# First normalisation of a hybrid encoder kernel: the inverse norms moved from a scaling pass into a diagonal matrix used in the turn

## The chip, the cores and the metric

One NeuronCore of one Trainium2 chip runs the whole program. The metric is the device time of one execution in microseconds (us), and the number that counts is the median over several runs. The engines are named PE (TensorE, matrix products; PEld is its weight load), DVE (VectorE), ACT (ScalarE), POOL (GpSimd) and SP (SyncE, which only issues transfers here).

## The reference, cut to what matters

```python
def rmsnorm(x, g):
    xf = x.astype(F32)
    y = xf * lax.rsqrt(jnp.mean(xf * xf, axis=-1, keepdims=True) + EPS)
    return (y * g.astype(F32)).astype(x.dtype)

def encoder_layer(x, mem, P, l):
    ...
    u = rmsnorm(x, P['norm_mix'][l])
    proj = u @ P['w_in'][l]
    ...
```

The model is one encoder layer on two groups of rows, 1024 prompt rows and 256 sample rows, each 1024 channels wide, in float32. What comes after the lines above (differential attention, a Hyena convolution, gates, cross-attention and a mixture of 16 experts) is not touched by the change. The first thing that the layer does is `u = rmsnorm(x, norm_mix)`: each row of `x` is divided by the root of its mean square and each channel is multiplied by a gain.

## The kernel before, in words

The rows of both groups form ten tiles of 128 rows (NT = 10). Most of the program is a long run of matrix products that want their inputs with channels on partitions. So the first stage must produce `UT`, the normalised and turned input: 8 blocks of 128 channels by 1280 rows. It starts from `XS`, in which the ten tiles lie as they come from memory, rows on partitions.

For each tile t the stage does five things, each on the engine that has it:

- SP loads the rows, two tiles to a transfer (`x_load`, line 429), ahead of the weights and tables that the next stages read. The transfers of the filter network's inputs and weights (`feat_in`, lines 452 to 455) and of the first projection weights (`hyena_load`, line 448) come behind them in the same queue.
- ACT squares the tile and sums it by row (line 1417), then takes the root of the mean (line 1419). This is `normed`; it counts in `norm_act`.
- DVE takes the reciprocal of the root (line 1739) and multiplies the tile's 1024 columns by it into one of two buffers `XN` (line 1745). This is `scaled`; it counts in `xn_ready`.
- PE turns the eight 128x128 blocks of `XN`, four into each of the banks 6 and 7 (`turn_rows`, line 763). The block is the stationary side and the identity matrix the moving one. It counts in `xn_tr`, one for each half.
- DVE multiplies each half (128x512) by the channels' gains on its way out of the bank into `UT` (`rows_in`, line 1752), which counts in `ut_ready`.

The order on DVE is written out in `norm_stage`: scaling of tile t+1 first, then the two halves of tile t. PE may turn half h of tile t+1 once DVE has emptied half h of tile t. DVE may write a buffer of `XN` once the turn of two tiles earlier is done with it.

```python
            wait("feat_in", 64)
            wait("ut_ready", 2 * NT)
            for n in range(3):
                filter_layer(0, n)
            for b in range(2 * HG):
                wait(f"hy_in_{b % 3}", 16 * (b // 3 + 1))
```

These lines (841 to 846) are what PE does next: it waits for the filter's inputs and for all twenty halves, does the first layer of the filter network (three products, line 747), and goes on to the projections of the Hyena branch (line 747 too, the line of the helper `product`). `norm_stage` is used for this first stage alone here; the later normalisations call `scaled`, `turn_rows` and `rows_in` themselves and are unchanged.

Of the kernel before, what the change touches and what calls it, by code (L numbers as in the profile page):

```python
# [11 lines left out]
ALU = mybir.AluOpType  # L12
# [3 lines left out]
P = 128  # L16
# [5 lines left out]
NT = NTP + NTS  # L22
# [22 lines left out]
V_MIX, V_X, V_MEM, V_FFN = 0, 8, 16, 24  # L45
# [62 lines left out]
class Count:  # L108
# [12 lines left out]
    def wait(self):  # L121
        self.eng.wait_ge(self.sem, self.base + self.n)
# [28 lines left out]
def encoder_kernel(nc, a, out_p, out_s):  # L151
# [9 lines left out]
    with ExitStack() as ctx:  # L161
        sem = {n: ctx.enter_context(nc.semaphore(n)) for n in SEMS}
        arena = ctx.enter_context(nc.sbuf_tensor("arena", [P, 204 * 256], F32))
        PS = ctx.enter_context(nc.psum_tensor("banks", [P, 8, 512], F32))

        def at(kb, *dims):

            n = int(np.prod(dims))
            v = arena[:, int(kb * 256):int(kb * 256) + n]
            if len(dims) == 2:  # L170
                v = v.rearrange("p (a b) -> p a b", a=dims[0])
            if len(dims) == 3:
                v = v.rearrange("p (a b c) -> p a b c", a=dims[0], b=dims[1])
            return v

        def small(name, shape, dt=F32):
            return ctx.enter_context(nc.sbuf_tensor(name, shape, dt))

        vec, ident, mirror = small("vec", [P, NV]), small("ident_sb", [P, P]), small("mirror_sb", [P, P])
        ones, eps = small("ones", [P, 2]), small("eps", [P, 1])  # L180
        stat = small("stat", [P, 3, 16])
# [13 lines left out]
        UT = at(0, KD, T)  # L195
        XS = at(80, NT, D)
        XN = [at(194 + 4 * i, D) for i in range(2)]
        SQJ = at(202, D // 2).bitcast(BF16)
        FEAT, H1, ARG, RND, H2 = at(60, T), at(65, T), at(70, T), at(75, T), at(140, T)
        W3F, W1F, W2F, VROW = at(145, 2 * HY), at(149, P), at(149.5, P), at(150, P)  # L200
# [75 lines left out]
        def bank4(b):  # L276
            return PS[:, b, :].rearrange("p (a c) -> p a c", a=4)

        def wide(v, n):

            return v.unsqueeze(2).to_broadcast([v.shape[0], v.shape[1], n])
# [44 lines left out]
        tiles = [slice(t * P, (t + 1) * P) for t in range(NT)]  # L326
# [96 lines left out]
        def _(sp):  # L423
# [146 lines left out]
            for t in range(NT):  # L570
# [3 lines left out]
                sp.wait_ge(sem["xn_ready"], N_FFN + t + 1)  # L574
                sp.dma_start(hn[tiles[t], :], XN[t % 2]).then_inc(sem[f"hn_out_{t % 2}"], 16)
                if t == NTP - 1:
# [166 lines left out]
        def _(pe):  # L743
            def product(out, pairs):

                for n, (l, r) in enumerate(pairs):
                    last = pe.matmul(out, l, r, start=(n == 0), stop=(n == len(pairs) - 1))  # L747
                return last

            def wait(name, v):  # L750
                pe.wait_ge(sem[name], v)
# [4 lines left out]
            def turn_rows(q):  # L756

                wait("xn_ready", q + 1)
                for half in range(2):
                    if q >= 1:  # L760
                        wait("ut_ready", 2 * (q - 1) + half + 1)
                    for k in range(4):
                        last = pe.transpose(PS[:, 6 + half, k * P:(k + 1) * P], XN[q % 2][:, tiles[4 * half + k]], ident[:, :])  # L763
                    last.then_inc(sem["xn_tr"], 1)

            for t in range(NT):
                turn_rows(t)

            def filter_layer(layer, n):

# [120 lines left out]
            for g in range(HG):  # L891
# [14 lines left out]
                for odd in range(2):  # L906
                    last = product(PS[:, 5, odd * P:(odd + 1) * P],
                                   [(KSS[:, 2 * odd + s, tiles[g]], INVS[:, 2 * odd + s, :]) for s in range(2)])
# [264 lines left out]
            for q in range(8):  # L1173
                m, n = q % 4, q // 4
# [134 lines left out]
            for m in range(NTP // 2):  # L1309
                last = pe.transpose(PS[0:2 * NE, 2, m * P:(m + 1) * P],  # L1310
                                    LG[:, 2 * m:2 * m + 2, :].rearrange("p h e -> p (h e)"), ident[:, :])
# [13 lines left out]
            for m in range(NTS):  # L1325
                last = pe.transpose(PS[0:NE, 5, m * P:(m + 1) * P], LG[:, NTP + m, :], ident[:, :])
# [82 lines left out]
        def _(act):  # L1409
            steps = Count(act, sem["norm_act"])  # L1410

            def normed(q, src):

                col = q % 16
                if q:
                    steps.wait()
                steps.inc(act.activation(SQJ, src, ACT.Square, accum_out=stat[:, 0, col:col + 1]))
                steps.wait()
# [268 lines left out]
            def fin_square(t):  # L1687
                act.wait_ge(sem[f"fin_in_{t // 2}"], 16)
                if t:
                    fin.wait()  # L1690
                fin.inc(act.activation(SQJ, FIN[t], ACT.Square, accum_out=stat[:, 0, t:t + 1]))

# [11 lines left out]
            act.wait_ge(sem["fin_rec"], 1)  # L1704
            fin.inc(act.activation(SQJ[:, 0:256], YS, ACT.Square, accum_out=LSUM[:, 0:1]))
            act.wait_ge(sem["fin_rec"], 2)
            fin.wait()
            fin.inc(act.activation(SQJ[:, 0:512], YP[:, 0:512], ACT.Square, accum_out=LSUM[:, 1:2]))
            act.wait_ge(sem["norm_mm"], 2)
            fin.inc(act.activation(LSUM[:, 3:4], PS[:, 0, 0:1], ACT.Sqrt, scale=1.0 / D, bias=eps[:, 0:1]))  # L1710
            act.wait_ge(sem["fin_rec"], 3)
            fin.wait()
            fin.inc(act.activation(SQJ[:, 512:1024], YP[:, 512:1024], ACT.Square, accum_out=LSUM[:, 2:3]))
            act.wait_ge(sem["fin_rec"], 4)
# [4 lines left out]
        def _(dve):  # L1719
# [11 lines left out]
            step = Count(dve, sem["dve_step"])  # L1731
# [3 lines left out]
            def scaled(q, src, stored):  # L1735

                dve.wait_ge(sem["norm_act"], 2 * q + 2)
                col = slice(q % 16, q % 16 + 1)
                step.inc(dve.reciprocal(stat[:, 2, col], stat[:, 1, col]))
                if q >= 2:  # L1740
                    dve.wait_ge(sem["xn_tr"], 2 * (q - 1))
                if stored and q >= N_FFN + 2:
                    dve.wait_ge(sem[f"hn_out_{q % 2}"], 16 * ((q - N_FFN) // 2))
                step.wait()
                dve.tensor_scalar(XN[q % 2], src, stat[:, 2, col], None, ALU.mult).then_inc(sem["xn_ready"], 1)

            def rows_in(q, dst, t, gain):

                for half in range(2):
                    dve.wait_ge(sem["xn_tr"], 2 * q + half + 1)  # L1750
                    g = vec[:, gain + 4 * half:gain + 4 * half + 4]
                    dve.tensor_tensor(dst[:, 4 * half:4 * half + 4, tiles[t]], bank4(6 + half), wide(g, P), ALU.mult).then_inc(sem["ut_ready"], 1)  # L1752

            def norm_stage(q0, n, src, dst, gain, stored=False):
                scaled(q0, src(0), stored)
                for t in range(n):
                    if t + 1 < n:
                        scaled(q0 + t + 1, src(t + 1), stored)
                    rows_in(q0 + t, dst, t, gain)

            norm_stage(0, NT, lambda t: XS[:, t, :], UT, V_MIX)

            def angles(layer):

# [118 lines left out]
            half = [HALF[:, m, :] for m in range(4)]  # L1883
# [41 lines left out]
            for g in range(HG):  # L1925
# [4 lines left out]
                for odd in range(2):  # L1930
                    for s, bank, c0, c1, o, n in ((0, 3 + odd, 0, 512, 0, LP), (1, 5, odd * P, (odd + 1) * P, LP, LS)):
                        dst, src = Z[:, g, o + odd:o + n:2], PS[:, bank, c0:c1]
                        if not odd and not s:
                            dst, src = dst.rearrange("p (i r) -> p r i", r=2), src.rearrange("p (r i) -> p r i", r=2)
# [248 lines left out]
            for q in range(8):  # L2183
                m, n = q % 4, q // 4
# [200 lines left out]
            for j in range(4):  # L2385
                if j:
                    step.wait()
                src = ident[:, CS * j:CS * (j + 1)]
# [13 lines left out]
            last = NE - 1  # L2402
# [40 lines left out]
def build(nc, arrays):  # L2443
    a = {n: nc.dram_tensor(f"in_{n}", v.shape, F32, kind="ExternalInput").ap() for n, v in arrays.items()}
    outs = [nc.dram_tensor(f"out_{i}", s, F32, kind="ExternalOutput").ap() for i, s in enumerate(_OUTS)]
    encoder_kernel(nc, a, *outs)
# [11 lines left out]
```

## Time and profile before

| | us |
|---|---|
| median of 3 runs | 2751.53 (2748.62 to 2759.06) |
| the profiled execution's own time | 2748.56 |
| its span, first to last instruction | 2746.8 |
| PE busy | 2641.3 (96%) |
| DVE busy | 878.5 (32%) |
| ACT busy | 418.1 (15%) |
| POOL busy | 251.4 (9%) |
| first product of the stage after the first normalisation | starts at 33.19 |

The profiled execution took 1.8 us more than its span, which is what lies before the first and behind the last instruction. It lies 3.0 us below the median of the three runs and beside the lowest of them. Times in the trace count from the span's start. A matrix product's duration covers its way through the array, so that successive ones overlap: the spacing of a group of n is (the group's time less one duration) / (n - 1).

### The profile page before, as it was taken

The numbers are of one execution on the slowest core, as the hardware profiler recorded it, in microseconds if no ns is written. First come the engines' busy times: TensorE is split into PE (matmuls) and PEld (weight loads), VectorE is DVE, ScalarE is ACT, GpSimd is POOL, SyncE is SP. The second block draws the span as 40 slices with busy tenths as digits, with TensorE's granted clock in tenths as the row PEclk, the third lists the DMA queues.
The fourth block names the chain that finished last, engine by engine and source line by source line (L and its number), as shares of the span: only waits on it lengthen the run. The fifth ranks groups of instructions, "written<-read, shape, count | busy, mean of one in ns | idle before, by whom it ended". The sixth has DMA issues, their size and how long they took to land.

```text
span 2746.8 us, 29882 instructions
## 1 busy us (share of the span) xinstructions
PE 2641.3 (96%) x12380; PEld 1780.4 (65%) x12380; DVE 878.5 (32%) x1512; ACT 418.1 (15%) x946; POOL 251.4 (9%) x270
## 2 busy tenths in 40 slices
PE   7999899999989999999999999978999999999997
PEld 4554454466657777765455486546888788788876
DVE  5566733166782111144200053271111111111112
ACT  3120000144451111102100032110000000000002
POOL 0120100000001010041000002000100110010001
PEclk9999999999999999999999999978999999999999
DMA  4110211000010010041111100137787787778776
GB/s 156 31 50 3 91 51 31 0 16 1 1 47 24 23 47 23 24 168 31 46 46 31 61 31 31 62 123 272 256 278 248 240 272 265 262 234 271 248 260 245
DMA packets 189938, 315.78 MB, mean 115 GB/s; under 512 B 6122, under 2 KB 69951, under 8 KB 189216
## 3 DMA queue, kind: packets, MB, share of 16 engines
q1 hardware_dynamic: 181952, 292.87, 31.1%
q0 software_dynamic: 7904, 21.76, 3.1%
q8 instruction: 58, 0.95, 0.1%
q14 instruction: 24, 0.20, 0.0%
HBM read 288.40 MB, written 26.21 MB: 115 GB/s over the span
## 4 chain that ended last, share of the span: by engine, by line
PE 90%; DVE 8%; ACT 1%; issue 1%; DMA 0%; POOL 0%; POOLq 0%; DVEq 0%; SPq 0%; ACTq 0%
PE banks L747 60%; PE banks L1029 9%; PE banks L928 5%; PE banks L1118 4%; PE banks L1243 3%; PE banks L948 2%; PE banks L1378 2%; DVE arena L1895 2%; PE banks L963 1%; PE banks L763 1%; PE banks L1348 1%; DVE arena L1752 0%; DVE arena L2279 0%; DVE arena L2282 0%; DVE att L1995 0%
## 5 line engine op out<-in xcount | busy, mean ns | idle before, releaser
L747 PE MATMUL banks<-arena 128*128 128x160 f32 (+3 forms) x8070 | 1754.2, 378 | 23.5 <-ACT arena L1449 8.1
L747 PEld LDWEIGHTS banks<-arena 128*128 128x128 f32 x8070 | 1245.9, 191 | 536.5 <-issue 479.4
L1029 PE MATMUL banks<-arena 128*128 128x320 f32 x896 | 243.5, 433 | 2.6 <-DVE arena L2031 2.1
L633 POOL TENSOR_TENSOR arena<-arena 128x512 f32<-128x512 f32 (+1 forms) x72 | 109.6, 1535 | 1294.8 <-DMA arena<-in_w_br_hyena 749.9
L1029 PEld LDWEIGHTS banks<-arena 128*128 128x128 f32 x896 | 169.7, 190 | 72.5 <-issue 2.3
L2362 DVE TENSOR_TENSOR arena<-arena,banks 128x160 f32<-128x160 f32 x128 | 41.1, 321 | 521.1 <-ACT arena L1679 488.7
L1679 ACT ACTIVATE arena<-banks 128x160 f32<-128x160 f32 x120 | 36.5, 304 | 773.2 <-PE banks L747 773.2
L928 PE MATMUL banks<-arena 128*128 128x512 f32 (+1 forms) x384 | 142.7, 521 | 2.5 <-DVE arena L1935 2.5
L1118 PE MATMUL banks<-arena 128*128 128x512 f32 x280 | 122.6, 593 | 0.7 <-ACT arena L1589 0.7
L1995 DVE TENSOR_REDUCE att<-banks 128x1 f32<-128x1024 f32 (+1 forms) x80 | 81.4, 1059 | 125.4 <-PE banks L948 125.3
L928 PEld LDWEIGHTS banks<-arena 128*128 128x128 f32 x384 | 70.5, 190 | 55.4 <-issue 52.4
L1243 PE MATMUL banks<-arena 128*128 128x512 f32 x224 | 100.8, 605 | 0.0
L1511 ACT ACTIVATE arena<-banks,att 128x1024 f32<-128x1024 f32 (+1 forms) x80 | 78.8, 986 | 116.6 <-DVE att L1995 116.6
L1118 PEld LDWEIGHTS banks<-arena 128*128 128x128 f32 x280 | 52.2, 190 | 61.8 <-issue 60.3
L948 PE MATMUL banks<-arena 64*128 64x512 f32 (+1 forms) x288 | 69.2, 594 | 13.1 <-ACT arena L1511 12.3
L2370 DVE TENSOR_SCALAR arena<-banks,gates 128x512 f32<-128x512 f32 x30 | 22.5, 751 | 173.4 <-PE banks L747 173.4
L1243 PEld LDWEIGHTS banks<-arena 128*128 128x128 f32 x224 | 43.0, 196 | 50.3 <-issue 50.3
L707 POOL TENSOR_TENSOR turn<-ones 128x1 f32<-128x1 f32 x15 | 2.9, 195 | 642.3 <-DVE arena L2373 642.3
L2176 DVE COPY arena<-banks 128x512 f32 (+1 forms) x8 | 5.5, 692 | 174.4 <-PE banks L747 174.4
L1378 PE MATMUL banks<-arena 128*32 128x256 f32 x1024 | 58.6, 380 | 0.8 <-DVE arena L2362 0.8
L948 PEld LDWEIGHTS banks<-arena 64*128 64x128 f32 x288 | 24.6, 186 | 51.6 <-issue 39.2
L2093 DVE TENSOR_TENSOR arena<-arena,banks 128x512 f32<-128x512 f32 x40 | 27.5, 687 | 88.9 <-PE banks L747 88.9
(241 smaller groups left out, 1596.7 us busy)
## 6 DMA issues: line engine op xcount, KB each, us to landing
arena<-in_w_exp_gate SPq DMA_DIRECT2D x32, 2048.0 KB, 8.0
arena<-in_w_exp_up SPq DMA_DIRECT2D x32, 2048.0 KB, 12.9
arena<-in_w_exp_down SPq DMA_DIRECT2D x32, 2048.0 KB, 18.1
arena<-in_w_in SPq DMA_DIRECT2D x36, 512.0 KB, 4.0
arena<-in_x_prompt SPq DMA_DIRECT2D x8, 1024.0 KB, 7.7
residual_rows<-arena SPq DMA_DIRECT2D x10, 512.0 KB, 2.6
normed_rows<-arena SPq DMA_DIRECT2D x10, 512.0 KB, 2.6
arena<-residual_rows SPq DMA_DIRECT2D x5, 1024.0 KB, 15.3
```

Source lines behind the costliest of these rows:

```text
L633: done.inc(pool.tensor_tensor(out, l, r, op))
L747: last = pe.matmul(out, l, r, start=(n == 0), stop=(n == len(pairs) - 1))
L928: last = pe.matmul(PS[:, job_bank(h, j), n * cn:(n + 1) * cn], WQK[h][part][:, k, :], UT[:, k, c0:c0 + cn], start=(k == 0), stop=(k == KD ...
L948: last = pe.matmul(PS[:, 2 * c + n // 512, 0:m], q[half, tiles[i]], k[half, k0 + n:k0 + n + m], start=True, stop=True, tile_position=(c * ...
L1029: last = pe.matmul(PS[:, 3 * (g % 2) + bank, 0:GN], l[:, k, :], r[:, k, :], start=(k == 0 and which in (G1, G2, G5)), stop=(k == 3), skip_ ...
L1118: last = pe.matmul(PS[:, bank, :], l[:, k, :], r[:, k, :], start=(k == 0 and which in (G1, G2, G5)), stop=(k == 3), skip_group_check=which ...
L1243: last = pe.matmul(PS[:, bank, :], l[:, k, :], r[k] if which == G7 else r[:, k, :], start=(k == 0 and which in (G1, G2, G5)), stop=(k == 3 ...
L1378: last = pe.matmul(PS[CS * j:CS * (j + 1), 5, 0:256], HE[:, f, CP:CE], WD[j // 2][:, f, (j % 2) * 256:(j % 2 + 1) * 256], start=(f == 0), ...
L1511: act.activation(PP[u % 2][c][:, 0:kn], s, ACT.Exp, bias=att[:, u % 2, 0, c:c + 1], accum_out=att[:, u % 2, 2, c:c + 1]).then_inc(sem["exp ...
L1895: spec.inc(dve.tensor_tensor(out, l, r, op))
L1995: dve.tensor_reduce(att[:, u % 2, 0, c:c + 1], s, AX.X, ALU.max, negate=True).then_inc(sem["smax_ready"], 1)
L2362: dve.tensor_tensor(HE[:, f, :], SL[:, f % 2, :], PS[:, f % 3, CE:2 * CE], ALU.mult).then_inc(sem["he_ready"], 1)
```

## The change

The scaling pass over the tile's 1024 columns is gone. In its place DVE multiplies the identity matrix (128x128) by the tile's inverse norms, one for each partition, into one of two buffers `ROOTS`; this is a diagonal matrix. PE no longer transposes a scaled tile: it multiplies the raw rows `XS` (stationary side) by the diagonal (moving side), which turns and scales at once. The eight products of a tile are plain matrix products now and not transposes. Counts, waits, banks and what follows each step are as they were; the buffers `ROOTS` lie where `XN` lay, and `XN` is still used by the later normalisations.

```diff
+        ROOTS = [at(194 + 4 * i, P) for i in range(2)]
...
+            def first_rows(t):
+
+                wait("xn_ready", t + 1)
+                for half in range(2):
+                    if t >= 1:
+                        wait("ut_ready", 2 * (t - 1) + half + 1)
+                    for k in range(4):
+                        last = pe.matmul(PS[:, 6 + half, k * P:(k + 1) * P], XS[:, t, tiles[4 * half + k]], ROOTS[t % 2],
+                                         start=True, stop=True)
+                    last.then_inc(sem["xn_tr"], 1)
+
             for t in range(NT):
-                turn_rows(t)
+                first_rows(t)
...
-            def norm_stage(q0, n, src, dst, gain, stored=False):
-                scaled(q0, src(0), stored)
-                for t in range(n):
-                    if t + 1 < n:
-                        scaled(q0 + t + 1, src(t + 1), stored)
-                    rows_in(q0 + t, dst, t, gain)
-
-            norm_stage(0, NT, lambda t: XS[:, t, :], UT, V_MIX)
+            def first_scaled(t):
+
+                dve.wait_ge(sem["norm_act"], 2 * t + 2)
+                step.inc(dve.reciprocal(stat[:, 2, t:t + 1], stat[:, 1, t:t + 1]))
+                if t >= 2:
+                    dve.wait_ge(sem["xn_tr"], 2 * (t - 1))
+                step.wait()
+                dve.tensor_scalar(ROOTS[t % 2], ident[:, :], stat[:, 2, t:t + 1], None, ALU.mult).then_inc(sem["xn_ready"], 1)
+
+            first_scaled(0)
+            for t in range(NT):
+                if t + 1 < NT:
+                    first_scaled(t + 1)
+                rows_in(t, UT, t, V_MIX)
```

On DVE, at the start of the first normalisation, the program before has these rows:

```order
L1739 RECIPROCAL stat<-stat 128x1
L1745 TENSOR_SCALAR arena<-arena,stat 128x1024
L1739 RECIPROCAL stat<-stat 128x1
L1745 TENSOR_SCALAR arena<-arena,stat 128x1024
L1752 TENSOR_TENSOR arena<-banks,vec 128x4x128 x2
```

and the changed one these:

```order
L1769 RECIPROCAL stat<-stat 128x1
L1773 TENSOR_SCALAR arena<-ident_sb,stat 128x128
L1769 RECIPROCAL stat<-stat 128x1
L1773 TENSOR_SCALAR arena<-ident_sb,stat 128x128
L1764 TENSOR_TENSOR arena<-banks,vec 128x4x128 x2
```

The order is the same; only the TENSOR_SCALAR is another, 128 columns of the identity for 1024 of the tile. `arena` is the large on-chip buffer in which nearly all tiles lie, `banks` the accumulation banks, `vec` the gains, `stat` the norms. On PE, from the start of the program:

```order
L754 MATMUL banks<-ident_sb,arena 128x88
L763 MATMUL banks<-ident_sb,arena 128x128 x80
L747 MATMUL banks<-arena 128x512 x2
L747 MATMUL banks<-arena 128x256
L747 MATMUL banks<-arena 128x512 x16
```

has become

```order
L755 MATMUL banks<-ident_sb,arena 128x88
L774 MATMUL banks<-arena 128x128 x80
L748 MATMUL banks<-arena 128x512 x2
L748 MATMUL banks<-arena 128x256
L748 MATMUL banks<-arena 128x512 x16
```

Again the count and the place are the same, and the operands are others. Nothing else differs on any engine but the line numbers.

## Rows read from the trace of the kernel before

**Rows 1.** The page: busy time by engine, and the chain that ended last

```profile
PE 2641.3 (96%) x12380; PEld 1780.4 (65%) x12380; DVE 878.5 (32%) x1512; ACT 418.1 (15%) x946; POOL 251.4 (9%) x270
...
PE 90%; DVE 8%; ACT 1%; issue 1%; DMA 0%; POOL 0%; POOLq 0%; DVEq 0%; SPq 0%; ACTq 0%
```

**Rows 2.** The chain in order of time: start us, us, what

```profile
28.22 0.61 DVE arena L1752
28.83 0.14 issue
28.97 0.64 PE banks L763 x4
29.61 0.74 DVE arena L1745
...
33.06 0.14 issue
33.19 1.11 PE banks L747 x2
...
35.20 61.29 PE banks L747 x168
```

**Rows 3.** Timeline of PE: start us, us, engine, line, operation [idle before]

```profile
11.73 1.97 PE L763 MATMUL banks<-ident_sb,arena 128*128 128x128 f32 x8 [2.85 <-DVE arena L1745]
13.92 1.94 PE L763 MATMUL banks<-ident_sb,arena 128*128 128x128 f32 x8 [0.21 <-DVE arena L1752]
...
18.26 1.23 PE L763 MATMUL banks<-ident_sb,arena 128*128 128x128 f32 x8 [0.21 <-DVE arena L1752]
...
26.84 1.84 PE L763 MATMUL banks<-ident_sb,arena 128*128 128x128 f32 x8 [0.47 <-DVE arena L1752]
28.97 1.16 PE L763 MATMUL banks<-ident_sb,arena 128*128 128x128 f32 x8 [0.29 <-DVE arena L1752]
31.09 1.16 PE L763 MATMUL banks<-ident_sb,arena 128*128 128x128 f32 x8 [0.96 <-DVE arena L1752]
```

**Rows 4.** Timeline of all engines: one lap of DVE, and ACT's last root

```profile
24.60 0.29 ACT L1419 ACTIVATE stat<-stat,eps 128x1 f32<-128x1 f32 x1
...
27.47 0.75 DVE L1745 TENSOR_SCALAR arena<-arena,stat 128x1024 f32<-128x1024 f32 x1
28.14 1.28 DVE L1752 TENSOR_TENSOR arena<-banks,vec 128x512 f32<-128x512 f32 x2
...
29.33 0.15 DVE L1739 RECIPROCAL stat<-stat 128x1 f32<-128x1 f32 x1
29.59 0.76 DVE L1745 TENSOR_SCALAR arena<-arena,stat 128x1024 f32<-128x1024 f32 x1
```

**Rows 5.** Groups of DVE in the whole trace: busy us, mean ns

```profile
L1745 DVE TENSOR_SCALAR arena<-arena,stat 128x1024 f32<-128x1024 f32 x34 | 25.7, 756 | 3.7
...
L2000 DVE TENSOR_SCALAR arena<-banks,att 128x128 f32<-128x128 f32 x40 | 13.8, 344 | 14.5 <-PE banks L747 14.5
...
L2335 DVE TENSOR_SCALAR arena<-arena 16x32 f32<-16x32 f32 x1 | 0.2, 169 | 0.0
```

**Rows 6.** Timeline of PE in the attention: plain products, then transposes

```profile
711.25 2.05 PE L747 MATMUL banks<-arena 128*128 128x128 f32 x16
713.14 1.04 PE L963 MATMUL banks<-ident_sb,arena 128*128 128x128 f32 x8
```

**Rows 7.** Busy us by stretch, with the granted clock (PEclk)

```profile
core 0: us, PE busy (x) PEld busy (x) DVE busy (x) ACT busy (x) POOL busy (x), PEclk, DMA share, GB/s
...
22.50:24.60 2.10, 1.16 (x8) 0.84 (x8) 1.99 (x5) 1.94 (x6) 0.00 (x0) 1.00 1.10 170
24.60:26.80 2.20, 1.65 (x8) 1.18 (x8) 2.09 (x5) 1.57 (x2) 0.00 (x0) 0.60 1.19 266
26.80:28.90 2.10, 1.84 (x8) 1.57 (x8) 1.99 (x5) 0.00 (x0) 0.00 (x0) 0.61 1.20 381
```

**Rows 8.** Timeline of PE, plain products of 512 columns: at half clock, at full

```profile
322.13 3.59 PE L747 MATMUL banks<-arena 128*128 128x512 f32 x4 [8.11 <-ACT arena L1449]
...
33.19 3.13 PE L747 MATMUL banks<-arena 128*128 128x512 f32 x7 [0.94 <-DVE arena L1752]
```

**Rows 9.** Granted clock at 318 to 325 us, by stretch

```profile
318.00:325.00 7.00, 2.87 (x4) 1.32 (x5) 5.52 (x11) 1.35 (x3) 4.24 (x4) 0.54 0.01 2
```

**Rows 10.** SP's queue at the start, and transfers' us from issue to landing

```profile
17.54 0.59 SPq L455 DMA_DIRECT2D arena<-in_filt_w  x1
18.17 2.15 SPq L448 DMA_DIRECT2D arena<-in_w_in  x2
...
arena<-in_w_in SPq DMA_DIRECT2D x2, 512.0 KB, 9.5
```

## The prediction

> **What bounds the kernel now.** I read the page first. PE is busy 96% of the span and makes 90% of the chain that ended last [rows 1], so a change to a stage of DVE and ACT can only matter where PE still waits. Then the chain in order of time: until 33.06 us it runs through the first normalisation, and what it shows there is mostly DVE, with four transposes at a time between [rows 2]. From 33.19 PE goes without a break that matters (one row of 61.29 us follows at 35.20). So all that can be won lies before 33.19, and what ends this stage earlier moves the rest of the program forward by as much.
>
> Inside the stage I read PE's timeline: a turn of eight transposes starts every 2.13 us (26.84, 28.97, 31.09), and whether it takes 1.84 or 1.16 us changes nothing in that pace [rows 3]. PE isn't the bound, then. DVE's timeline gives the reason [rows 4]: from one scaling to the next (27.47 to 29.59) are 2.12 us, made of the scaling up to the start of the evictions (0.67; they begin 0.08 before its recorded end), the two evictions up to the next reciprocal (1.19), and from there to the next scaling 0.26. DVE has no gap. I call this a lap.
>
> **The scaling.** 1024 columns take 0.75 us [rows 4], [rows 5]. No row shows 128 columns of on-chip memory by a norm of each partition. From below: 16x32 elements take 0.169. From above: 128x128 out of the banks takes 0.344. Both are in [rows 5]. I take 0.23, on the line between 0.169 at 32 columns and 0.756 at 1024 (0.169 + 96 x 0.587 / 992), because the 1024-column row is the same operation from the same memory. So 0.52 us less in each scaling, and a DVE lap of 2.13 - 0.52 = 1.61 (1.55 to 1.72 by the two ends). Reciprocals, evictions and the hand-over between them stay.
>
> **The products.** 80 transposes become 80 plain products. In the attention 16 plain ones of 128x128 take 2.05 us and 8 transposes 1.04 [rows 6]. One lasts about 0.28, so the spacing is (2.05 - 0.28) / 15 = 0.118 against (1.04 - 0.27) / 7 = 0.110. That is 0.03 for a half of four, 0.06 for a tile.
>
> The Trainium skill ("TensorE: Matmul & The Clock Gate", Terms) says that the transpose mode of trn2 is four times faster for fp32, and its "FP8 and Floating Point Precision" (TensorE Precision Notes) that true fp32 takes four passes. The rows just read don't agree with that as a ratio between these two instructions; what it would do is rival 3.
>
> **Does PE still fit?** From DVE's release of a half: 0.14 until PE starts, 0.64 for four transposes, 0.61 for the eviction [rows 2]. With 0.03 more that is 1.42, under 1.61 by 0.19: hidden. But this holds only at 2.4 GHz. The first turns are slow: eight take 1.97 and 1.94, and from 18.26 on 1.23 and then 1.16 [rows 3]. That is the 1.2 GHz level, by a spacing of (1.94 - 0.43) / 7 = 0.22, twice 0.110, though the granted clock has no record there. At 1.2 GHz four plain products take about 1.12, and the loop of a half 0.14 + 1.12 + 0.61 = 1.87: **PE takes over as the bound** in the cold turns, which were covered by 2.13 before.
>
> **The sum, as starts of turns.** Turn 0: 11.73 - 0.52 = 11.21. Turn 1: 13.92 - 0.52 = 13.40, for DVE does the scaling of tile 1 ahead of the evictions of tile 0, and that scaling still waits for the same root of ACT. Turns 2 and 3 at 1.87: 15.27, 17.14. Turn 4, with the clock up at about 18.2 as before: 18.9. Turns 5 to 9 at 1.61: 20.5, 22.1, 23.7, 25.3, 26.9. From the last turn's start to the first product of the next stage 33.19 - 31.09 = 2.10 stays, two evictions and two hand-overs: 29.0. **Gain 33.19 - 29.0 = 4.2 us.**
>
> ACT is not touched. Its last root ends at 24.89 [rows 4]; reciprocal and diagonal until 25.4, a first eviction and the hand-over 0.75: turn 9 can't start before 26.2, and starts at 26.9. So ACT is not the bound, but only 0.7 us away. With the scaling at 0.17 the gain is 4.7, at 0.34 it is 3.2 (nine of them on the path).
>
> **What waits behind.** PE next wants the filter's inputs. No row has their landing. The last of them is issued at 17.54, ahead of two transfers of 512 KB issued at 18.17 which land about 9.5 us after issue [rows 10], so by about 27.7 in the order of the queue, 1.3 us before I need them. The first projection weights were issued still earlier. No transfer is added, moved or passed by another in any queue, and POOL and SP have no step in the change. The transfers that later stages ask for are released by PE's counts, so they move along.
>
> Against the profiled execution this is 2748.6 - 4.2 = 2744.4. That execution lies 3.0 below the median of the three runs; against the median the forecast is 2751.5 - 4.2 = **2747.3**.
>
> **Rival 1: the products bring the clock up sooner.** The granted clock falls to about half, 0.60 and 0.61, from 24.6 to 28.9, after three turns in which PE was busy 1.16 of 2.1 us [rows 7]. With laps of 1.61 PE is busy 1.2 of 1.61, so I don't expect that fall in my sum. If moreover the rise comes two turns earlier, the laps of 1.87 become 1.61, 0.8 us in all, up to ACT's limit at 26.2: gain 4.9, 2746.6. For it: PE is busier from the first turn on. Against: PE was already busy 1.94 of 2.19 us in the cold turns and still had to wait until 18.2.
>
> The Trainium skill (same page on TensorE, Part 4) says that transposes don't count as busy for the clock; by it, plain products alone would warm PE, which is this rival. The trace disagrees in part: the rise at 18.2 came with nothing but transposes before it.
>
> **Rival 2: the clock falls all the same.** Before, the fall cost nothing, for laps of 2.13 cover a slow PE [rows 3]. At the same place it now costs a lap of 1.87 for 1.61 and a slower last turn, 0.7 us in all: gain 3.5. If it comes after 29.0 it meets products of 512 columns, which take 3.59 for four at half clock ([rows 8], clock 0.54 in [rows 9]) against 3.13 for seven: half of some 3.4 us is lost, 1.7, so the gain is 2.5 and the time 2749.0.
>
> **Rival 3, slower: plain products of raw rows are streamed four times.** Spacing 0.44 warm and 0.88 cold. Turn 0 would fill 11.2 to 18.2, nine more take 3.5 each: the next stage starts near 50.6, +17.4 us, 2768.9. It decides once eight take over 2.13, a spacing of 0.27. Rows 6 speak against it with 0.118; what is left is that no row shows a raw tile against a diagonal.
>
> **Rival 4: nothing comes through.** The filter's inputs land later than the order of the queue says, or a wait further on takes the gain. Time 2751.5. The long unbroken row after 35.20 speaks against it [rows 2].
>
> **Chances.** Forecast 0.60, rival 1 0.12, rival 2 0.20, rival 4 0.05, rival 3 0.03. Half a percent, 13.8 us, is about what a measurement of this kernel can tell from no change. The whole stage from turn 0 on is 21.5 us and ACT alone sets 26.2 for its last turn, so a gain over 13.8 is in none of the cases; I leave 0.01 to it. Slower by over half a percent is rival 3. All others are within: 0.96.
>
> The range holds the four likely cases (2746.6 to 2751.5) and the scatter of a median: the runs lie 2.9 below and 7.5 above theirs. Down: 2746.6 less 2.9, about 2743.5. Up: 2749.0 and half of 7.5, about 2753.
>
> **What would show it.** The TENSOR_SCALAR of 128x128 near 0.23 us; turns about 1.9 apart at first and 1.6 after the clock's rise; the first product of 512 columns near 29.0; PE idle before each turn shrinking from 0.96 to some 0.4 once warm; everything after it unchanged but for the shift. Wrong would be: products further apart than 0.13 when warm, a start that stays at 33, PE waiting for a DMA at the filter's first layer, or laps that stay at 2.1 because the small operation isn't shorter.

## The result, and the profile after

The changed kernel takes 2756.88 us (median of 20 runs, 2754.12 to 2763.88); the kernel before, timed on the same chips, 2751.14 (20 runs, 2748.09 to 2759.21). The ratio is 1.0021, with a 95% interval of 1.0012 to 1.0030: slower by 5.7 us. The forecast was 4.2 us faster, with an upper end of 2753.0. The move is under the half per cent named there, but it is clear of noise and has the other sign.

The profiled execution took 2759.98 us, 3 above its own median. The page's busy times, to be read against [rows 1]:

```profile
PE 2655.7 (96%) x12460; PEld 1792.9 (65%) x12460; DVE 879.2 (32%) x1512; ACT 418.0 (15%) x946; POOL 250.9 (9%) x270
...
PE 90%; DVE 7%; ACT 1%; issue 1%; DMA 0%; POOL 0%; POOLq 0%; DVEq 0%; SPq 0%; ACTq 0%
```

PE has 12460 matmuls for 12380, and as many more weight loads: **80 more, though the program has as many products as it had transposes.** The chain in order of time (start us, us, what), the part that answers to [rows 2]:

```profile
10.94 0.30 DVE arena L1773
11.23 0.04 issue
11.28 21.40 PE banks L774 x160
32.68 0.02 issue
32.70 0.70 DVE arena L1764
33.40 0.14 issue
33.54 1.11 PE banks L748 x2
```

The 80 products are 160 records, and they are the chain from end to end. DVE, which set the pace before, now waits. Its timeline for a lap shows that (start us, us, engine, line, operation, [idle before]):

```profile
27.30 0.15 DVE L1769 RECIPROCAL stat<-stat 128x1 f32<-128x1 f32 x1
27.56 0.29 DVE L1773 TENSOR_SCALAR arena<-ident_sb,stat 128x128 f32<-128x128 f32 x1
27.80 0.69 DVE L1764 TENSOR_TENSOR arena<-banks,vec 128x512 f32<-128x512 f32 x1
28.69 0.69 DVE L1764 TENSOR_TENSOR arena<-banks,vec 128x512 f32<-128x512 f32 x1 [0.20 <-PE banks L774]
29.30 0.15 DVE L1769 RECIPROCAL stat<-stat 128x1 f32<-128x1 f32 x1
```

A lap is 2.00 us for 2.13. The small scaling takes 0.29 for 0.75, and the rest of what it saves is spent on waiting for PE. The next stage starts at 33.54 for 33.19 in this pair, and at 33.5 to 34.6 in the runs below: the stage gives nothing.

That is 0.35 us, not the 5.7 of the medians or the 11.4 between these two executions. To find the rest I took the start of the same PE instruction in both traces, counted from the end of the program, and subtracted. The difference is 0.3 at 310 us, 1.4 at 335, 3.1 at 420, 4.8 at 545, 6.3 at 780, 8.4 at 1200, 10.0 at 1730 and 11.4 at 1880; between 1750 and 1790 it is 11.7, and otherwise it is flat from step to step. The steps are of two kinds. The first is the granted clock. These stretches of the kernel before:

```profile
core 0: us, PE busy (x), PEclk, DMA share, GB/s
310.00:330.00 20.00, 11.89 (x33) 0.83 0.20 32
405.00:435.00 30.00, 25.02 (x86) 1.00 0.28 73
525.00:550.00 25.00, 20.52 (x83) 1.00 0.00 0
760.00:780.00 20.00, 15.28 (x94) 1.00 0.29 76
```

stand in the changed one as:

```profile
310.00:330.00 20.00, 12.09 (x31) 0.74 0.20 31
405.00:435.00 30.00, 25.02 (x83) 0.94 0.32 92
525.00:550.00 25.00, 20.52 (x70) 0.93 0.00 1
760.00:780.00 20.00, 17.01 (x87) 0.91 0.01 1
```

At each of these places PE is idle for 2 to 8 us, and in the changed kernel's execution the clock goes to its 1.2 GHz level there, while in the other it does not (at 310 to 330 it falls in both, and for longer in the changed one). Below, such a stretch at 1.2 GHz is called a spell; one costs up to 1.7 us. The second kind is a collision. POOL's additions on `w_out` start when its transfer is in, and DVE's additions beside them slow down (before, then after):

```profile
1180.56 0.69 DVE L2093 TENSOR_TENSOR arena<-arena,banks 128x512 f32<-128x512 f32 x1 [2.30 <-PE banks L747]
1181.28 0.42 DVE L2095 TENSOR_TENSOR arena<-arena 128x256 f32<-128x256 f32 x1
1181.51 22.58 POOL L633 TENSOR_TENSOR arena<-arena 128x2048 f32<-128x2048 f32 x7 [61.01 <-DMA arena<-in_w_out]
...
1184.01 0.69 DVE L2093 TENSOR_TENSOR arena<-arena,banks 128x512 f32<-128x512 f32 x1 [2.31 <-PE banks L747]
...
1184.73 1.63 DVE L2095 TENSOR_TENSOR arena<-arena 128x256 f32<-128x256 f32 x1
```

```profile
1186.45 26.60 POOL L634 TENSOR_TENSOR arena<-arena 128x2048 f32<-128x2048 f32 x10 [59.66 <-DMA arena<-in_w_out]
1186.87 0.69 DVE L2111 TENSOR_TENSOR arena<-arena,banks 128x512 f32<-128x512 f32 x1 [2.31 <-PE banks L748]
...
1187.59 3.66 DVE L2113 TENSOR_TENSOR arena<-arena 128x256 f32<-128x256 f32 x1
```

The same DVE addition takes 0.42 us alone and 1.63 to 4.02 beside POOL. How long depends on how far POOL is in an addition of its own. The first of them alone, in the changed kernel:

```profile
1186.45 4.51 POOL L634 TENSOR_TENSOR arena<-arena 128x2048 f32<-128x2048 f32 x1 [59.66 <-DMA arena<-in_w_out]
```

It ends at 1190.96, and the DVE addition that started beside it at 1187.59 ends at 1191.25. In all 14 traces of this study each of the four long DVE additions ends 0.28 to 0.29 us behind the POOL addition in which it began. So the collision is in the kernel before too: there the four take 1.63, 2.77, 4.02 and 4.02 us, in the changed one 3.66, 4.02, 4.02 and 4.02. What differs is how early in POOL's first addition DVE's falls: in the kernel before POOL starts just behind the start of a short DVE addition and the next one comes 3.2 us later; in the changed one it comes 1.1 us after POOL's start. The issue of `w_out` and what moved beside it gives the reason for that. The kernel before, then the changed one (first the issue, then the queues between issue and POOL's start):

```profile
1166.74 0.37 SPq L523 DMA_DIRECT2D arena<-in_w_out  x1
...
q1 hardware_dynamic: 2080, 4.19, 77.8%
q8 instruction: 1, 0.02, 0.5%
```

```profile
1173.05 0.37 SPq L524 DMA_DIRECT2D arena<-in_w_out  x1
...
q1 hardware_dynamic: 2080, 4.19, 87.0%
```

POOL starts 14.8 us after the issue before and 13.4 after. In the kernel before a transfer of instructions moves in the same time as `w_out`; in the changed one it doesn't. The queue's transfers are of 16384 bytes, some 256 PE records apart in the trace, and the page counts 58 of them before and 59 after, so I take them to be PE's instructions. The 160 more PE instructions (80 matmuls, 80 weight loads) move these transfers against the program. `w_out` comes sooner, and the kernel loses 2.1 us by it.

### The profile page after: what moved, and what is told of

The parts are those of the page before. It is cut to its first block, busy times and chain, and to the rows that moved or that the text cites. A ratio compares the mean times of both kernels' runs of the same rounds, so it can differ in the third digit from the quotient of the medians.

```text
span 2758.2 us, 30042 instructions
## 1 busy us (share of the span) xinstructions
PE 2655.7 (96%) x12460; PEld 1792.9 (65%) x12460; DVE 879.2 (32%) x1512; ACT 418.0 (15%) x946; POOL 250.9 (9%) x270
## 4 chain that ended last, share of the span: by engine, by line
PE 90%; DVE 7%; ACT 1%; issue 1%; DMA 0%; POOL 0%; POOLq 0%; DVEq 0%; SPq 0%; ACTq 0%
PE banks L748 60%; PE banks L1041 9%; PE banks L940 5%; PE banks L1130 4%; PE banks L1255 4%; PE banks L960 2%; PE banks L1390 2%; DVE arena L1913 2%; PE banks L975 1%; PE banks L774 1%; PE banks L764 1%; PE banks L1360 1%; DVE arena L2113 1%; DVE arena L2297 0%; DVE arena L2300 0%
```

## The experiments

Each was timed in 12 runs (alternate: 9) beside the kernel before, whose median was 2749.7 in the first group (before_again, after_again, turn_raw, plain_ident), 2750.8 in the second (after_pad96, before_pad160, before_late, alternate), 2750.9 in the third (before_split, turn_raw_again) and 2755.6 in the last (before_split2, before_pad256). Each group ran on another chip, and the median moves from one to the next by as much as the effect looked for; whether the chip or the clock's spells move it is not separated. The kernel before's 133 runs in the whole study fall in two clusters: 74 lie below 2751.7 and 59 at 2753.8 and above. Its two traces are both of the lower cluster, so what its long runs lose, and where, no trace shows. So a ratio is given with its interval, and rows of the trace bear the verdicts.

**1 and 2. Both kernels once more**, unchanged.

> The kernel before, unchanged, to see how much of the difference between two profiled executions belongs to the change. Theory A (the plain product is two instructions, each as long as a transpose, and costs 0.35 us in this stage; the rest of the 5.7 us is where short spells of half clock and a collision of POOL with DVE near 1185 us fall, which differ from one execution to the next): first product of the next stage at 33.2 us again, but spells of half clock at other places than in the first profile, and the POOL additions at another distance from the transfer's issue than 14.8 us; time 2748 to 2759. Theory B (everything behind the stage is fixed by the program): spells at 267, 318 and 1745 us again, and the same 14.8 us.

> The changed kernel again. Both theories: first product of the next stage at 33.5 us, 160 PE records in the first stage. Theory A: the spells of half clock at 413, 540 and 772 us are not all there again, and the ratio to before may come nearer to 1.000 than 1.002. Theory B: the three spells are there again and the ratio is 1.002 again, so that the change has a fixed cost of some 5 us behind the stage.

before_again: ratio 0.9995 (0.9983 to 1.0007), `w_out` ready after 14.7 us, no step anywhere behind 34 us against the first trace. after_again: 2756.59, ratio 1.0020 (1.0008 to 1.0033); of the three spells one (near 540) is there again, the other two aren't; `w_out` ready after 13.6 and 2.3 us lost at 1182 to 1200 again. So the loss in the median is there again, as theory B had it, and A's "by chance" falls for it; but its parts differ: the collision is the same both times, the spells not.

**3. Transposes of the raw tile**, the diagonal made and not read, so that this kernel leaves out the normalisation by rows.

```diff
-                        last = pe.matmul(PS[:, 6 + half, k * P:(k + 1) * P], XS[:, t, tiles[4 * half + k]], ROOTS[t % 2],
-                                         start=True, stop=True)
+                        last = pe.transpose(PS[:, 6 + half, k * P:(k + 1) * P], XS[:, t, tiles[4 * half + k]], ident[:, :])
```

> The changed kernel with transposes of the raw tile against the identity in place of the products with the diagonal; the diagonal is still made, and not read. So the normalisation by rows is left out of the first stage. Theory A: eight transposes are eight PE records and not sixteen; DVE paces with a lap of 2.13 - 0.46 = 1.67 us; the next stage starts near 29.7 us, 3.5 us sooner than before. Rival (the small scaling or the waits hold the stage, not the products): it stays near 33.5 us.

> The kernel turn_raw once more. If its 11 of 12 runs above 2750 were a chance of where the clock's spells stood in that session, over half of the runs now lie at 2744.4 to 2746.5 (the kernel before's fast group less 3.65). If a start of the long part 3.65 us sooner goes with more spells, they lie at 2750 to 2756 again.

PE's and DVE's timeline in the warm part:

```profile
22.47 1.16 PE L774 MATMUL banks<-ident_sb,arena 128*128 128x128 f32 x8 [0.50 <-DVE arena L1763]
...
22.84 0.15 DVE L1768 RECIPROCAL stat<-stat 128x1 f32<-128x1 f32 x1
23.10 0.29 DVE L1772 TENSOR_SCALAR arena<-ident_sb,stat 128x128 f32<-128x128 f32 x1
...
23.30 1.28 DVE L1763 TENSOR_TENSOR arena<-banks,vec 128x512 f32<-128x512 f32 x2
...
24.13 1.16 PE L774 MATMUL banks<-ident_sb,arena 128*128 128x128 f32 x8 [0.50 <-DVE arena L1763]
```

Eight records and a lap of 1.66, and the next stage starts at 29.55, 4.0 us sooner than with the products (33.54). The DVE side of my sum was right. Yet the total hardly follows: 2752.74 (ratio 0.9999, 0.9987 to 1.0011), and 2750.71 the second time (0.9988, 0.9977 to 0.9999). Of the 24 runs 5 lie at 2744.5 to 2745.1, which is about the kernel before's usual lowest (2748.0) less 3.6, though 2 of its own 133 runs, both in the last group, reach 2745.1 and 2746.1. The other 19 runs are longer, and both traces, which are of these, show spells. In the second trace the shift is 3.8 us of gain at 405, 1.2 at 760 and 1.9 of loss at the end. The gain is real in the stage, and in both traces it is taken back by spells; why more often than in the kernel before is open. So with no more PE instructions than before, too, the rest of the program lost 8.2 us in the first trace and 5.9 in the second.

**4. Plain products of the scaled tile against the identity**, the full scaling kept.

```diff
-                        last = pe.transpose(PS[:, 6 + half, k * P:(k + 1) * P], XN[q % 2][:, tiles[4 * half + k]], ident[:, :])
+                        last = pe.matmul(PS[:, 6 + half, k * P:(k + 1) * P], XN[q % 2][:, tiles[4 * half + k]], ident[:, :],
+                                         start=True, stop=True)
```

> The kernel before with its full scaling pass, but with plain products of the scaled tile against the identity in place of transposes. It computes what the reference does. Theory A: 160 PE records, eight products take about 2.0 us when warm; DVE's lap of 2.13 us covers most of it, so the next stage starts between 33.2 and 34.5 us. If the cost behind the stage (5 us) comes with plain products or their rounding, it shows here too: 2754 to 2764 us. If it comes by chance of the clock's spells, the time is within 2748 to 2762 without a fixed offset.

160 records again, whatever the operands. The next stage starts at 36.66, over 2 us later than expected: a lap is 2.21 us, as both engines wait for each other in turn, and PE's first turns are at the 1.2 GHz level. Total 2760.07, ratio 1.0026 (1.0014 to 1.0039): 3.5 in the stage, and `w_out` ready after 13.4 with 2.2 us lost beside POOL.

**5, 6 and 7. Only the number of PE instructions.** One product of one column is four instructions (two weight loads, two matmuls); 24, 40 or 64 of them stand at the very start, while PE waits for its first data, and their result is not used. The edit with 24:

```diff
+            wait("vec_zero", 1)
+            for _ in range(24):
+                pe.matmul(PS[0:1, 1, 0:1], ones[:, 0:1], ones[:, 0:1], start=True, stop=True)
             wait("vec_in", 16 * 12)
```

> The changed kernel with 96 more PE instructions while PE has nothing to do: 24 products of one column at the very start (4 instructions each, results unused). With the 160 that the change adds to PE (two weight loads and two matmuls for each plain product instead of one and one) that is 256 instructions, one whole 16 KB instruction transfer, so that the instruction transfers stand against the program as in the kernel before. Theory F (a part of the loss behind the first stage is the place of PE's instruction transfers): w_out is ready for POOL 14.8 us after its issue as in the kernel before and not 13.4, the number of DVE additions of about 4 us beside POOL is 2 whole ones and no more than 3 long, and the 2.1 to 2.3 us lost between 1182 and 1200 us in all three runs with plain products are not lost. First product of the next stage stays at 33.5 to 34.6. Total 2 to 5 us under the changed kernel's 2756.6: 2751 to 2755. Rival C (plain products themselves, or the half-clock spells alone): 13.4 us and the loss at 1182 stay, 2756 to 2757.

> The kernel before with 160 more PE instructions at the very start (40 products of one column, results unused), as many as the change adds, and nothing else. Theory F: w_out is ready 13.4 us after its issue, four long DVE additions beside POOL, 2.1 to 2.3 us lost near 1182 to 1200, although no product of the first stage has changed; total 2752 to 2756. Rival C: like the kernel before, 2749.7 (up to 1 us more if the padding delays the first turn).

> The kernel before with 256 more PE instructions at the very start (64 products of one column), one whole instruction transfer. Theory F (what counts is where PE's instruction transfers stand, not that the program is longer or that PE worked at the start): w_out ready after 14.8 us, POOL's collision as in the kernel before, total like the kernel before, within 1 us of its median, unlike before_pad160 with fewer extra instructions, which lost 5.6. Rival (more instructions or early PE work cost the time): 2756 or more.

| kernel | PE instructions more than before | median, us | ratio (95%) | `w_out` ready after |
|---|---|---|---|---|
| changed | 160 | 2756.59 | 1.0020 (1.0008 to 1.0033) | 13.6 |
| before_pad160 | 160 | 2756.35 | 1.0017 (1.0004 to 1.0029) | 13.3 |
| after_pad96 | 256 | 2750.73 | 1.0005 (0.9993 to 1.0018) | 14.7 |
| before_pad256 | 256 | 2749.12 | 0.9986 (0.9976 to 0.9996) | 14.5 |

**The loss goes with the place of PE's instruction transfers, not with the products.** The kernel before with 160 idle instructions, no product of the stage changed and the next stage starting at 33.11, has a median as slow as the changed one's. The changed kernel with 96 more is as fast as the kernel before, and before_pad256, which has more PE work at the start than before_pad160, isn't slow either. The size is less sure than the direction: the intervals of before_pad160 and after_pad96 overlap, both medians lie 0.3 outside the ranges that I had given, and the lowest run of before_pad160 is 2751.39, while none of the changed kernel's 32 runs is under 2753.95. In before_pad160 POOL again starts ahead of a DVE addition:

```profile
1188.50 18.47 POOL L633 TENSOR_TENSOR arena<-arena 128x2048 f32<-128x2048 f32 x4 [59.50 <-DMA arena<-in_w_out]
1189.06 0.69 DVE L2096 TENSOR_TENSOR arena<-arena,banks 128x512 f32<-128x512 f32 x1 [2.30 <-PE banks L747]
1189.78 3.52 DVE L2098 TENSOR_TENSOR arena<-arena 128x256 f32<-128x256 f32 x1
```

and between issue and POOL's start no instruction transfer is in the queues; in after_pad96 there is one again (the line that before_pad160 lacks stands second). Over all traces the split is clean: the 9 with an instruction transfer between the issue and POOL's start have 14.5 to 14.9 us between them, the 5 without one 13.3 to 13.6.

```profile
q1 hardware_dynamic: 2080, 4.19, 79.4%
q8 instruction: 1, 0.02, 0.4%
```

One point is against a simple tale. before_pad256 is the fastest by its median, yet its trace has the early collision, and a worse one, by a hair: POOL starts at 1181.57 and the DVE addition at 1181.66.

```profile
1181.57 22.50 POOL L633 TENSOR_TENSOR arena<-arena 128x2048 f32<-128x2048 f32 x7 [60.71 <-DMA arena<-in_w_out]
1181.66 4.70 DVE L2098 TENSOR_TENSOR arena<-arena 128x256 f32<-128x256 f32 x1
```

It loses 3.1 us there, has 3.4 at 1760, and is back at 0.2 by 1830, because the spells between 1745 and 1790 lie otherwise than in the kernel before. My expectation for this run was wrong on the collision; its total is what I expected only against the 2749.7 of the first group, for in its own group the kernel before stood at 2755.6. Gains and losses don't add up along this program; each shifts what the clock does behind it.

**8. A pure shift of all that follows**: two more writes on DVE (128x1280 and 128x512) ahead of the last evictions.

```diff
+                    if t == n - 1:
+                        step.inc(dve.memset(RND, 0.0))
+                        step.inc(dve.memset(ARG[:, 0:512], 0.0))
+                        step.wait()
                     rows_in(q0 + t, dst, t, gain)
```

> The kernel before with two extra writes on DVE (128x1280 and 128x512, about 1.7 us) ahead of the last tile's evictions: a pure shift of all that follows by 1.7 us, with the program on PE unchanged. If the half-clock spells fall by chance of the execution, the median is 1.7 above the kernel before, 2751.4, and runs at 2749.8 to 2751.5 are as frequent as those at 2748.1 to 2749.8 in the kernel before (over half). If a spell's place depends on how the program stands against its own start, the spread changes: few such runs, and a median 3 to 6 us above, as turn_raw showed none but one of 12 runs at its expected 2745.

2757.74 (2750.83 to 2763.66), ratio 1.0021 (1.0008 to 1.0034). In its trace the next stage starts at 34.75, 1.6 us late, and by 60 us it is 2.9 late, after a stretch at 33.0 to 38.5 with a clock of 0.69. 5 of 12 runs stand at 2750.8 to 2751.6, where a mere shift of 2.9 puts them (the trace, of 2751.54, is one of these, with no further step), and 7 at 2757.2 and above. The ones of the first group say that a shift can cost just itself; the median says that it need not. This kernel has as many PE instructions as the one before and `w_out` ready after 14.9 us, and its median is as slow as the changed kernel's: a median alone can't tell the instruction transfers from another shift, and only the rows can.

**9. Scaling and product in turn**, even tiles as before and odd ones by the diagonal (PE's part of the edit; DVE's writes the scaled tile or the diagonal to match).

```diff
-                        last = pe.matmul(PS[:, 6 + half, k * P:(k + 1) * P], XS[:, t, tiles[4 * half + k]], ROOTS[t % 2],
-                                         start=True, stop=True)
+                        out, block = PS[:, 6 + half, k * P:(k + 1) * P], tiles[4 * half + k]
+                        last = (pe.matmul(out, XS[:, t, block], ROOTS[1], start=True, stop=True) if t % 2 else
+                                pe.transpose(out, XN[0][:, block], ident[:, :]))
```

> A version that could beat both: even tiles scaled and turned as before, odd tiles by the product with the diagonal. It computes what the reference does. The laps alternate between DVE-bound ones (0.75 for the scaling) and PE-bound ones; from DVE's rows (2.13 and 1.67) and PE's (8 transposes 1.16, 16 records 2.0) a pair should take 3.8 to 4.0 us against 4.26: next stage at 31.5 to 32.3 us. Total by theory A with 80 more PE instructions: 1 to 2 us under the kernel before if the instruction transfers and spells behind stay as they are, and up to 5 over it if they fall badly.

A pair takes 3.96 us, as expected, but the stage ends at 33.98 and not at 32: the first product tile runs at the 1.2 GHz level (3.72 us for its 16 records), and the last tile, an odd one, has DVE waiting for its products. With 80 more instructions it also has `w_out` ready after 13.5 us and the collision: 2762.96, ratio 1.0035 (1.0022 to 1.0048).

**10 and 11. A delay in the middle**, five extra products at about 1204 us, whose result the next one overwrites; of 512 columns in before_split, as here, and of 256 in before_split2.

```diff
+                if i == 0 and which == G1:
+                    for _ in range(5):
+                        pe.matmul(PS[:, bank, :], l[:, 0, :], r[:, 0, :], start=True, stop=True)
```

> The kernel before with five extra products of 512 columns (20 PE instructions, 2.1 us of PE time, results overwritten) at about 1204 us, ahead of the first output projection: the same delay at the same place that the earlier w_out and POOL's collision cause in the kernels with 160 more PE instructions, with the first 1200 us as in the kernel before. Theory S (the delay costs its 2.1 us, and moreover moves the low-activity stretches of 1700 to 1880 us against those of 270 to 800, so that one or the other meets more spells of half clock): w_out ready after 14.8 us, few or no runs under 2752, median 2753 to 2757. Rival (only the delay itself counts): the kernel before's runs plus 2.1: over half of the runs at 2750.2 to 2752, median 2752.

> before_split with the delay that was meant: the five extra products have 256 columns, so they take 2.1 us and not the 4.3 us that ten records of 512 columns took in before_split. Theory S (a delay of 2.1 us at 1204 us costs more than itself, because no standing of the clock's spells then suits both the stretch of 270 to 800 us and that of 1700 to 1880): of the runs at 2750.2 to 2752.2 (the kernel before's fast group plus 2.1), which are over half of the kernel before's, few or none are left; median 2753.5 to 2757. Rival (only the delay counts): median 2752 to 2753 and half of the runs at 2750.2 to 2752.2.

In the first I made the mistake of the prediction again: a product of 512 columns is two records of 0.43 us, so the delay was 4.3 us and not 2.1. It gave 2756.76, ratio 1.0018 (1.0008 to 1.0028), lowest 2753.72; the kernel before's runs between 2748.0 and 2750.3, which are 59 of the 133 timed in this study, would with 4.3 more lie at 2752.3 to 2754.6, and 1 of 12 does. Its trace, though, is 5.5 us behind the kernel before's already at 1200 us, ahead of the added products, by spells between 310 and 780 us, where the program is still the kernel before's. The second has the delay that was meant (the traces differ by 2.72 us just ahead of it, spells again, and 4.88 just behind) and takes 2755.23, ratio 1.0015 (1.0003 to 1.0028), against a kernel before which in this group stood at 2755.56. At 2750.2 to 2752.4 lies 1 of 12. Both medians agree with theory S, that a delay there costs more than itself, but with such a spread from group to group, and with losses ahead of the delay in both traces, they don't prove it.

## Why the prediction was wrong

- **"80 transposes become 80 plain products ... 16 plain ones of 128x128 take 2.05 us": the step that failed.** The row's x16 counts records, and I read it as products. The attention has 8 such products in each unit: the program's order on PE shows this, and the timeline has 8, 16 and 8 records for these three lines.

```
L948 MATMUL banks<-arena 128x512 x4
L747 MATMUL banks<-arena 128x128 x8
L963 MATMUL banks<-ident_sb,arena 128x128 x8
```

  Eight products are sixteen records in [rows 6], eight transposes are eight. A float32 product costs 2 x 0.118 = 0.236 and a transpose 0.110, a factor of 2.1. The Trainium skill speaks of four passes ("FP8 and Floating Point Precision", TensorE Precision Notes) and of a transpose mode four times faster ("TensorE: Matmul & The Clock Gate", Terms); the runs show neither nearly equal costs, as I took it, nor a factor of four.
- **"Does PE still fit?"** With 0.236 four products take about 1.1 us and the loop of a half comes to 0.14 + 1.1 + 0.6 = 1.84, over my DVE lap of 1.61, and the sixteen records of a tile alone take 16 x 0.118 = 1.89: PE is the bound warm as well as cold, the lap measured 2.00, and the gain in the stage is nothing, where I had 4.2 us. Rival 3 had the place, the sign and the deciding spacing (0.27 for a lap of 2.13; 0.236 stays just under it), but with 0.44 nearly twice the spacing, and with 17.4 us a price that nothing here comes near.
- **"The scaling"** was right in kind and small in error: 0.29 for 0.23. turn_raw shows the lap that follows, 1.66 for 1.61, and a start of the next stage at 29.55 for 29.0.
- **"No transfer is added, moved or passed by another in any queue"** was wrong by the queue that carries PE's own instructions: I had taken it that their number stays, since products and transposes are as many. The stage by itself stands 0.35 us behind the kernel before; the rest of the 5.7 us comes behind it, 2.1 of them from this.
- **"What ends this stage earlier moves the rest of the program forward by as much"** was wrong in general: turn_raw started the rest 3.6 us sooner, and its two medians are 3.0 above and 0.2 below the kernel before's. The rest holds a collision that hangs on tenths of a microsecond, and stretches of little PE work that meet or don't meet a spell of half clock.
- Rival 2 (spells) was right as a mechanism, but I looked for them in and right behind the stage; the ones that matter lie at 310 to 780 and at 1700 to 1880 us. Rival 1 has no support: the rise of the clock came anywhere between 14 and 20 us, with transposes or products.
- ACT and the filter's inputs hold nothing up, as predicted: in turn_raw the turns and the first product of the next stage, at 29.55, still wait for DVE alone.

Shown: the two records, PE as the stage's bound, and that 160 idle PE instructions without any other change make the kernel slower (by 5.6 us in the medians; 1.1 to 8.0 by the interval), while 256 do not, nor do 96 on top of the changed kernel's 160. Shown in every trace with 80 or 160 more instructions (5 of 5): the early `w_out` and the 2.0 to 2.3 us beside POOL; in the 9 other traces the loss is there once (before_pad256). Not settled: how the remaining 3 us split over the clock's spells, and whether and why their place goes with the program's timing from its start; the low end of before_pad160 leaves room for a part that comes from the stage and not from the instruction transfers. No kernel of the study beats the one before by more than its own scatter with the reference's result; before_pad256 (0.9986) is the kernel before with its instruction transfers elsewhere, measured in a group in which the kernel before did badly.

## What to carry to other kernels

Count a row's xN against the program's own list before dividing by it; on PE in float32 a plain product is two weight loads and two matmuls and a transpose one of each, so "let the turn do the scaling" buys DVE time with as much PE time again. When a change alters the number of PE's instructions, its instruction transfers land elsewhere among the data transfers; pad to the same place to tell that from the change itself. A gain under some 5 us in this kernel has to be shown in its stage's rows, since the total answers to alignments.

## What the runs showed of the hardware that I had not expected

- Instruction transfers on PE matter: one inside the transfer of `w_out` (4.19 MB) goes with a readiness 14.5 to 14.9 us after the issue (9 traces), none with 13.3 to 13.6 (5 traces).
- An earlier transfer can cost time: 1.4 us sooner on POOL lost 2.1 us on PE. A DVE addition of 0.42 us that starts beside POOL's of 128x2048 (4.5 to 4.7 us) ends 0.28 us behind it, so that it takes up to 4.7 us.
- The same program can meet different spells of half clock from one execution to the next (the changed kernel's two traces do, the two of the kernel before do not), 1.5 to 1.7 us each where PE is dense. In the traced kernels with 80 or 160 more instructions the sum of all steps behind the stage was 7 to 14 us, in the kernel before 0 in both traces.
